# Per-result evictions, earlier weight casts, and dense steps placed ahead of side steps in a three-layer transformer kernel

## The reference

```python
# layer 1: three mixers side by side, gated and merged, then a feed-forward block
proj = rmsnorm(x) @ w_in
y_a = chunked attention with a relative bias, 8 heads of 64
y_b = gated linear recurrence (HGRN2) over chunks of 64, 8 heads of 64   # "the recurrence"
y_c = latent attention with rope, 8 heads
merged = sum_n sigmoid(gate_n) * (y_n @ w_branch[n]);  x = x + merged @ w_out
x = rmsnorm(x + relu(rmsnorm(x) @ w_ff1)**2 @ w_ff2)
# layer 2: stick-breaking attention, 16 heads of 64, then a SwiGLU block (2816 wide)
# layer 3: differential attention, 8 heads of 2 x 64, then a SwiGLU block
```

## Time and profile before

| what | us |
|---|---|
| median of 3 runs (2318.68 to 2321.15) | 2320.13 |
| the profiled execution's own time | 2320.95 |
| its span, first to last instruction | 2319.2 |
| PE busy (10484 matmuls) | 2247.8 |
| DVE busy | 1230.4 |
| ACT busy | 925.3 |
| POOL busy | 222.4 |

### The profile page before, as it was taken

The page is one execution under the profiler, slowest core; times in us unless marked ns, Lnnn a source line. Parts: engine busy times, 40 slices in busy tenths (PEclk is TensorE's granted clock), DMA queues, the critical chain, the costliest instruction groups (busy, mean ns, idle before and its releaser), DMA issues.

```text
span 2319.2 us, 26916 instructions
## 1 busy us (share of the span) xinstructions
PE 2247.8 (97%) x10484; PEld 1750.4 (75%) x10484; DVE 1230.4 (53%) x1859; ACT 925.3 (40%) x1537; POOL 222.4 (10%) x314
## 2 busy tenths in 40 slices
PE   7999899999999999999998999999999898999999
PEld 6767678667888888877565688888886666888887
DVE  4583564555544444463434555455545675555554
ACT  4353333444443233243544443333444565433332
POOL 0000221121200000031323200000120101000000
PEclk9999999999999999999999999999999999999999
DMA  4212111112322322322110122232221111322323
GB/s 159 80 39 91 46 36 62 66 37 91 109 91 100 100 91 100 100 80 75 37 55 28 64 100 94 97 100 92 99 91 64 55 55 55 100 100 91 100 91 109
DMA packets 52111, 187.48 MB, mean 81 GB/s; under 512 B 5905, under 2 KB 6033, under 8 KB 51857
## 3 DMA queue, kind: packets, MB, share of 16 engines
q1 hardware_dynamic: 51984, 185.76, 24.0%
HBM read 183.64 MB, written 2.10 MB: 80 GB/s over the span
## 4 chain that ended last, share of the span: by engine, by line
PE 91%; ACT 3%; DVE 3%; issue 1%; DMA 0%; POOL 0%; SPq 0%; DVEq 0%; ACTq 0%; POOLq 0%
PE ps L891 22%; PE ps L894 22%; PE ps L892 22%; PE ps L912 4%; PE ps L915 3%; PE ps L913 3%; PE ps L876 2%; PE ps L1003 2%; PE ps L975 1%; PE ps L1117 1%; PE ps L1233 1%; PE ps L1084 1%; PE ps L1209 1%; PE ps L1025 1%; PE ps L1221 1%
## 5 line engine op out<-in xcount | busy, mean ns | idle before, releaser
L891 PE MATMUL ps<-hh,wl 128*128 128x512 f32 x1408 | 567.9, 403 | 22.0 <-DVE wl L1614 12.8
L1614 DVE TENSOR_TENSOR wl<-raw,wh 128x1024 fp32r<-128x1024 f32 (+1 forms) x336 | 418.3, 1245 | 267.8 <-ACT wh L1285 267.7
L894 PE MATMUL ps<-hl,wh 128*128 128x512 f32 x1408 | 550.9, 391 | 0.0
L892 PE MATMUL ps<-hh,wh 128*128 128x512 f32 x1408 | 550.3, 391 | 0.0
L1285 ACT CAST wh<-raw 128x1024 fp32r<-128x1024 f32 (+1 forms) x336 | 350.4, 1043 | 388.8 <-PE ps L894 311.8
L891 PE MATMUL ps<-R,wl 128*128 128x512 f32 x896 | 361.7, 404 | 23.6 <-DVE x L1822 10.7
L894 PE MATMUL ps<-R,wh 128*128 128x512 f32 x896 | 352.3, 393 | 0.1
L892 PE MATMUL ps<-R,wh 128*128 128x512 f32 x896 | 351.7, 393 | 0.0
L891 PEld LDWEIGHTS ps<-hh,wl 128*128 128x128 f32 x1408 | 266.1, 189 | 83.0 <-issue 28.0
L894 PEld LDWEIGHTS ps<-hl,wh 128*128 128x128 f32 x1408 | 265.3, 188 | 56.9
L892 PEld LDWEIGHTS ps<-hh,wh 128*128 128x128 f32 x1408 | 265.8, 189 | 55.3 <-issue 3.1
(11 more groups left out here) (230 smaller groups left out, 2273.6 us busy)
## 6 DMA issues: line engine op xcount, KB each, us to landing
raw<-in_weights SPq DMA_DIRECT2D x332, 512.0 KB, 3.2
x<-in_x_t SPq DMA_DIRECT2D x4, 512.0 KB, 7.6
F<-in_x_t SPq DMA_DIRECT2D x4, 512.0 KB, 4.5
out<-x SPq DMA_DIRECT2D x8, 256.0 KB, 2.0
raw<-in_weights SPq DMA_DIRECT2D x4, 416.0 KB, 3.1
x<-in_bias SPq DMA_DIRECT2D x1, 1024.0 KB, 7.4
C<-in_consts SPq DMA_DIRECT2D x1, 832.0 KB, 6.5
F<-in_weights SPq DMA_DIRECT2D x2, 384.0 KB, 3.8
```

The source lines that it names most:

```text
L891: pe.matmul(out, lo[:, k, cs], xh, start=k == 0, stop=False)
L892: pe.matmul(out, hi[:, k, cs], xh, start=False, stop=False)
L894: last = pe.matmul(out, hi[:, k, cs], xl, start=False, stop=k == u.nk - 1)
L1614: dve.tensor_tensor(lo, src, hi.bitcast(F32), ALU.subtract).then_inc(S[name], 1)
```

## The change

Results of a unit get an `ev` step each, right behind the piece that ends them. The cast of chunk n+2 is put at the end of chunk n, ahead of the eviction in the same tick, instead of at the first piece of chunk n+1. Squares and low parts of a normed `out` unit come one tick behind its eviction (`ev_low`). `later` is kept in order of its counts. In the recurrence and in both stick-breaking stages the rest of a dense tick comes ahead of the side step (`ahead=False`). In the first differential group an empty side tick follows each of n = 3, 7, 11 and 15, and 31 instead of 27 side ticks are spread over the 48 dense ones.

```diff
-def interleave(main, side, ratio):
+def interleave(main, side, ratio, ahead=True):
...
                 products, rest = t
                 yield products, []
+                if not ahead:
+                    yield [], rest
+                    rest = []
...
+    def defer(self, n, *step):
+        self.later.append([n, step])
+        self.later.sort(key=lambda d: d[0])
...
     def lead(self, units, a, b):
         for u in units:
             self.place(u)
             for j in range(u.n):
-                rest = self.low()
-                if a == j == 0 and u is units[0]:
-                    rest += self.split(u.chunks[0] + 1)
-                if b == u.nk and j == u.n - 1:
-                    rest += self.split(u.chunks[0] + 2) + [("ev", u)]
+                rest = self.low() + self.due()
+                if b == u.nk:
+                    rest += self.ready(u, j)
                 yield [("mm", u, 0, j * u.nk + a, j * u.nk + b)], rest
 
+    def ready(self, u, j):
+        steps = (self.split(u.chunks[0] + 2) if j == u.n - 1 else []) + [("ev", u, j)]
+        if u.ev == "out" and u.arg["norm"] is not None:
+            self.defer(1, "ev_low", u, j)
+        if u.ev == "up" and u.arg["n"] == 2:
+            self.defer(2 if u.arg["m"] < 4 else 1000, "merge", u.arg["m"] + j)
+        if u.arg.get("ship"):
+            self.defer(2, "ship", u, j)
+        if u.ev in ("bq", "bg"):
+            self.defer(1, "ev2", u)
+        return steps
...
     def dense(self, units, more=None):
...
-                if piece[1] == 0:
-                    tick += self.split(u.chunks[piece[0]] + 1)
-                if piece == pieces[-1]:
-                    tick.append(("ev", u))
...
+                if u.kind == "rows" and piece[2] % u.nk == 0:
+                    tick += self.ready(u, piece[2] // u.nk - 1)
+                if u.kind == "cols" and piece[2] == 8:
+                    tick += self.split(u.chunks[piece[0]] + 2)
+                    if piece[0] == 3:
+                        tick.append(("ev", u))
+                        if u.ev == "dq":
+                            self.heads(u)
                 yield [("mm", u, *piece)], tick
...
     def diff(self, d):
...
+            if d.g == 0 and n < 16 and n % 4 == 3:
+                yield []
...
-        self.run(interleave(self.dense(uGA, {...}), iter(recurrence[:-4]), 49 / 48))
+        self.run(interleave(self.dense(uGA, {...}), iter(recurrence[:-4]), 49 / 48, False))
...
-        self.run(interleave(self.dense(uq[1][:3] + uk[1][:3]), iter(first[:17]), 17 / 24))
+        self.run(interleave(self.dense(uq[1][:3] + uk[1][:3]), iter(first[:17]), 17 / 24, False))
...
-        self.run(interleave(self.dense(uq[1][3:] + uk[1][3:] + uoS[0]), iter(second[1:]), 18 / 24))
+        self.run(interleave(self.dense(uq[1][3:] + uk[1][3:] + uoS[0]), iter(second[1:]), 18 / 24, False))
...
-        self.run(interleave(iter(made[44:92]), iter(first), 27 / 48))
+        self.run(interleave(iter(made[44:92]), iter(first), 31 / 48))
...
-        if u.ev == "out" and u.arg["norm"] is not None:
-            for j in range(u.n):
-                at.wait_ge("ev_d", u.dve[j])
-                normed_high(u.arg["norm"], u.arg["m"] + j)
-            for j in range(u.n):
-                squares(u.arg["norm"], u.arg["m"] + j)
-            return
...
+            elif u.ev == "out" and u.arg["norm"] is not None:
+                at.wait_ge("ev_d", u.dve[j])
+                normed_high(u.arg["norm"], u.arg["m"] + j)
...
+    def ev_low(u, j):
+        squares(u.arg["norm"], u.arg["m"] + j)
```

More of the change, by code:

```diff
@@ L288, in lead, with heads @@
             for j in range(u.n):
-                rest = self.low()
-                if a == j == 0 and u is units[0]:
-                    rest += self.split(u.chunks[0] + 1)
-                if b == u.nk and j == u.n - 1:
-                    rest += self.split(u.chunks[0] + 2) + [("ev", u)]
-                yield [("mm", u, 0, j * u.nk + a, j * u.nk + b)], rest
+                rest = self.low() + self.due()
+                if b == u.nk:
+                    rest += self.ready(u, j)
+                yield [("mm", u, 0, j * u.nk + a, j * u.nk + b)], rest
+    def ready(self, u, j):
[9 more added lines that the diff above has]
+        return steps
+    def heads(self, u):
+        self.defer(1, "dn_rope", u)
+        for tt in range(4):
+            self.defer((1, 1, 2, 3)[tt], "dn_sq", u, tt)
+            self.defer((2, 2, 3, 4)[tt], "dn_sum", u, tt)
+            self.defer((6, 6, 7, 7)[tt], "dn_mul", u, tt)
+            self.defer(9 + tt, "dt", u, tt)
+        self.defer(5, "dn_root", u)
     def dense(self, units, more=None):
@@ L510, in make @@
         recurrence = list(self.hgrn())
-        self.run(interleave(self.dense(uGA, {i: [("bf", uF[1], i)] for i in range(4)}), iter(recurrence[:-4]), 49 / 48))
+        self.run(interleave(self.dense(uGA, {i: [("bf", uF[1], i)] for i in range(4)}), iter(recurrence[:-4]), 49 / 48, False))
         self.banks = (0, 1, 4, 5)
@@ L573, in count @@
                 u = step[1]
-                for j in range(u.n):
+                for j in step[2:] or range(u.n):
                     if u.ev in ("qsplit", "bq", "bg", "gate", "fgate", "fup"):
@@ L1329, in merge, with ev @@
         act.copy(B.tile(("merged", 1), m)[0], B.xt(m)).then_inc(S["h_hi"], 1)
-    def ev(u):
+    def ev(u, *js):
         if u.ev in ("bq", "bg", "gate", "fgate"):
             return sigmoid(u)
-        if u.ev == "out" and u.arg["norm"] is not None:
-            for j in range(u.n):
-                at.wait_ge("ev_d", u.dve[j])
-                normed_high(u.arg["norm"], u.arg["m"] + j)
-            for j in range(u.n):
-                squares(u.arg["norm"], u.arg["m"] + j)
-            return
-        for j in range(u.n):
+        for j in js or range(u.n):
             bank = B.bank[u.banks[j]]
@@ L1793, in ev, with ev_low @@
                 ev_out(u, j, bank)
-        if u.ev == "out" and u.arg["norm"] is not None:
-            for j in range(u.n):
-                normed_low(u.arg["norm"], u.arg["m"] + j)
+    def ev_low(u, j):
+        normed_low(u.arg["norm"], u.arg["m"] + j)
     def tile_low(u, w):
@@ L2143, in ev, with ev_low @@
                 x_done[m] = plan.x_added[u.arg["n"], m]
-            if u.ev == "out" and u.arg["norm"] is not None and 1 <= u.arg["m"] + j < 7:
-                add_squares(u.arg["norm"], u.arg["m"] + j)
+    def ev_low(u, j):
+        if 1 <= u.arg["m"] + j < 7:
+            add_squares(u.arg["norm"], u.arg["m"] + j)
     def add_squares(v, m):
@@ L2354, in again, with ship @@
                      dram["x"][:, i * 1024:(i + 1) * 1024]).then_inc(S[f"xr{i}"], 16)
[L2356 to L2360, removed]
+    def ship(u, j):
+        ms = slice((u.arg["m"] + j) * T, (u.arg["m"] + j + 1) * T)
+        at.wait_ge("ev_d", u.dve[j])
+        sp.dma_start(dram["out"][:, ms], B.x[:, ms]).then_inc(S["out"], 16)
     todo = {"begin": begin, "split": split, "late": late, "c_turn": c_turn, "c_kt": c_kt, "again": again, "ship": ship}
```

6 lines of the change are left out of this document (3 added, 3 removed).

## The result

The changed kernel takes 2292.09 us (median of 4 runs, 2291.07 to 2296.73), the kernel before 2320.61 in the same comparison. The ratio is 0.9882 with a 95% interval of 0.9865 to 0.99: 1.2% faster. Forecast were 2287 us and a range of 2277 to 2305. The profiled execution's span is 2290.4 us.

What follows compares the result with a forecast made beforehand. PE, busy 97% of the span, was taken to bound the kernel. Gains in waits and clock less costs summed to 34.3 us off 2320.95, giving 2286.7, set at 2287; range 2277 to 2305.

Steps and rivals of the forecast that it cites:

- Evictions: Stick-breaking, recurrence, mixer C: PE's waits for `out` and `up` evictions go, 10.7 + 5.0 + 1.3 us.
- Casts: Issue waits at weight chunks: the recurrence's first gains 1.9 us, the other five go; sum 8.2 us.
- The wait of 3.03: At 1943.24, behind the differential's norm: only the last part goes, 1.0 us, bounds 0 and 3.0.
- The one at 36.75: At 36.75 the cast passes two copies, gaining 1.2 of 2.19 us.
- Mixer C's: Evictions wait for the moved cast, the norm starts later, PE already waits 0.85 us behind it: 1.6 us lost.
- Gates: 44 dense gate units, 0.07 us to spare: moved cast costs 0, bounds 0 and 0.97 each.
- The rival's price: SwiGLU gates: cast fully in series loses 44 x 0.97 = 42.7 us, giving 2330; chance 0.05.
- The side chain: Between side steps: 2.0 us of new PE waits, bounds nothing and 12; rival 12 us, 2301, chance 0.20.
- the rival's 12.6 us: Recurrence: all 12 low parts lengthen by 1.05 us meeting POOL on the shared port, at most 12.6 us.
- Differential attention: First group's empty side ticks and moved casts: 5.3 - 3.3 = 2.0 us gained, bounds -4 and +7.3.
- The clock: Granted clock falls behind six long waits go, wholly or half: 8.5 us gained, bounds 0 and 10.2.
- The sum: Whole kernel: all terms together take 34.3 us from 2320.95, giving 2286.7, forecast 2287.

Runs made afterwards that it cites:

- e4: Changed kernel with dense casts, low parts and evictions behind the side step again in the recurrence and stick-breaking: 2290.17 us.
- e5: Changed kernel with the results of a unit evicted together at its end again: 2296.65 us.
- e9: Changed kernel with results evicted together and dense work behind the side step again, early casts kept: 2315.78 us.
- e12: The changed kernel itself measured once more, two runs: 2294.38 us.
- e10: Changed kernel with the next weights' cast run twice at each of the 44 SwiGLU gate chunks, ahead of the sigmoid: 2335.43 us.
- e6: Changed kernel with the cast of the next weights back at the first piece of the chunk behind: 2302.78 us.
- e2: Changed kernel with each of the four empty steps given the masks, maxima and exponentials of the 512-key item just scored: 2285.05 us.
- e1: Changed kernel with the first differential group at its old pace, 27 side steps to 48 main steps, no empty steps: 2287.28 us.

## Why the prediction came out, step by step

**Evictions: right, for a reason half as wide as told.** All 17.0 us of bank waits went. The prediction gave both edits as the cause. e4, e5 and e9 show that either one is enough in the stages whose order was changed. The two waits elsewhere (1.33 in mixer C, 1.21 in the second differential group) needed the evictions one by one.

**Casts: right.** The first issue wait is 1.52 us (predicted 1.6), the other five left 0.33, so 9.8 - 1.85 = 7.95 us against 8.2. The wait of 3.03 is now 2.25 and named issue: 0.8 against 1.0 (it was 0.76 in e12, at the lower clock). The one at 36.75 fell from 2.19 to 0.21, 2.0 against 1.2. Mixer C's is 2.29, 1.4 worse than 0.85, against 1.6. But the clock's fall behind it wasn't in the sum.

**Gates: right.** 222 matmuls in 50 us, room 0.12 us where it was 0.07. The rival's price, 0.97 for each gate if the cast were in series, was a good one: e10 paid 0.98. It lost because the first cast lies beside DVE's scaling, as argued.

**The side chain: mis-sized, on the good side.** I took 2.0 us of new waits. There is one, 1.31 us behind four ACT instructions (a cast and a sigmoid) in the recurrence, and 2.7 us of POOL waits went: 1.4 gained. That was luck: the prediction didn't count the POOL waits, they stay away in e4, e6 and e9 as well, and what took them away stays open. Two waits of norms for POOL's sums, 1.17 and 0.66, are new and were nowhere in the sum.

**Port: the rival's 12.6 us did not come.** In the recurrence one low part of eleven (the prediction had twelve) took 2.10 us, the other full-size ones 1.22 to 1.26. It is the one that started inside a multiplication of POOL:

```profile
265.43 1.28 POOL L2195 TENSOR_TENSOR W<-F 128x512 f32<-128x512 f32 x1 [6.28 <-ACT F L1514]
265.70 2.10 DVE L1636 TENSOR_TENSOR wl<-raw,wh 128x1024 fp32r<-128x1024 f32 x1
```

POOL's runs to 266.71, so 1.01 us of it were left. The multiplication at 279.51 started inside the low part of 278.80, which took 1.25; there POOL's took 1.66, the longest of the stage, where the others took 1.27 to 1.56. No other low part of the stage shares more than 0.12 us with POOL. So few met POOL, and not each meeting lengthened the low part. The Trainium skill, page "SBUF — State Buffer", section "SBUF: two separate sides", says that the loser of the shared port pair waits until the other's instruction ends. The trace is near that: 1.01 + 1.22 = 2.23 against 2.10. But the length of one meeting says nothing about how many there will be.

**Differential attention: the step that failed.** "An empty side tick there makes it three ticks: 4.5 us go." Instead L1479's waits rose from 7.3 to 9.8 (forecast: to about 3), and ACT's evictions from 1.3 to 3.3: 4.5 us lost where 2.0 gained were forecast, 6.5 us of error, a little beyond the bound of 4 us lost. A step gives time only to work that is in a queue ahead of it. e2 shows it: the same spacing with the work moved into the step, and the three long waits are gone.

**Tail: missed.** 1.16 us, SP's order. The prediction didn't look at what `ship` per result is queued ahead of.

**The clock: mis-sized.** 8.5 us predicted; 11.9 - 6.9 = 5.0 in the first profile, and 11.9 - 10.2 = 1.7 in the second of the same kernel. It was worked out from the falls that go, and left out the ones that come. All six that it named went, 10.2 us and not 8.5; three of 1.7 us came, behind mixer C, at 1740 and at 1795. The falls also don't all repeat from one execution to the next.

**The sum.** Waits: 25.8 us forecast, 20.4 came (the differential 6.5, tail 1.16 and POOL 1.83 short; side chain 3.4 and start 0.8 over). Clock: 8.5 against 5.0. The other 8.4 - 5.0 = 3.4 us of busy time had no term in the prediction. About 2 us of it follow from e10, by an estimate: it shows that a wait costs 0.16 + 0.08 = 0.24 us beyond its idle time, and there are nine waits fewer (35 above 0.12 us, where there were 44). The rest stays open. So 2292.09 against 2287 is right within its range, but partly by luck: errors of both signs met.

Three experiments undo the change in parts: the banks 23.7 us (e9), the casts 10.7 (e6), the differential pace -4.8 (e1), together 29.6 against 28.5 measured. The closeness is in part chance. e9 also pays 2.2 us more in waits for POOL's sums than the changed kernel does (4.0 against 1.8), e6 also pays for late squares with late casts, and counted from e12 on its chip the first two are 21.4 and 8.4.

## What to carry to other kernels

To give a chain of dependent work more time, find the step in which each of its instructions is *queued*, on every engine; spacing that leaves them behind other work makes them later. Two edits that are made together should each be undone alone: here one of a pair was idle (the order around the side step), and another (late squares) was harmful without its partner (early casts). When a transfer or an eviction is split into smaller steps, look at what each is now queued ahead of, SP included.

## What was not expected of the hardware

- The same kernel with nearly the same waits had 6.9 and 10.2 us of clock loss in two profiles. A wait of 1.78 us was followed by a fall in one (0.93 and 0.73 in two windows) and by none in the other. A clock term from one profile is good to some 3 us here, 0.14% of the time.
- Idle PE of 0.68 us at a restart cost 0.93 to 0.98 us of time, as the profile counts a matmul 0.39 us long where the next starts 0.23 us behind it.
- In the recurrence a low part and a POOL multiplication overlapped by more than 0.12 us twice, and each time the one that started second was long: 2.10 us where 1.22 to 1.26 is usual on DVE, 1.66 where POOL shows 1.27 to 1.56.
